# Paired retention scores, norms moved behind the gates, and the second layer's norm factor applied after its projections

## The reference, cut to what matters

```python
# block 1: retention, 8 heads, q and k 64 wide, v 128 wide, chunks of 64
y_ret = retention_chunkwise(rq, rk, rv)       # = ((q k^T) * decay) v, decay[h] over the distance
y_ret = y_ret * lax.rsqrt(jnp.mean(y_ret * y_ret, axis=-1, keepdims=True) + EPS)   # per head
y_ret = from_heads(y_ret) * ret_norm_g[layer]
y_ret = (jax.nn.silu(r_g) * y_ret) @ w_ret_out[layer]
...
# end of block 1 and start of block 2
h = h + hierarchical_moe(hn, ...)
x = rms_norm(h, norm_final_g)                 # first block's last norm
h = rmsnorm(x, norm_mix_g)                    # second block's first norm
proj = h @ w_in                               # q_nope, q_rope, c_kv, k_rope, q_idx, k_idx, w_idx, q k v of b
q_idx, k_idx, q_rope, k_rope, q_b, k_b = rope(...) of their parts
```

## Time and profile before

| | |
|---|---|
| median of 3 runs | 1814.61 us (1813.84 to 1815.03) |
| profiled execution, its own time | 1821.67 us |
| its span | 1819.9 us |
| PE busy | 1664.2 us, 91% |
| DVE, ACT, POOL busy | 898.9, 748.2, 662.7 us |
| granted clock over the span | 0.965 |
| retention on PE | 316.2 to 363.7 us of the span |
| combine, up to the first key tile | 918.7 to 981.4 us |

### The profile page before, as it was taken

The page is one execution under the profiler, slowest core; times in us unless marked ns, Lnnn a source line. Parts: engine busy times, 40 slices in busy tenths (PEclk is TensorE's granted clock), DMA queues, the critical chain, the costliest instruction groups (busy, mean ns, idle before and its releaser), DMA issues. The chain is left out here.

```text
span 1819.9 us, 21002 instructions
## 1 busy us (share of the span) xinstructions
PE 1664.2 (91%) x7928; PEld 1339.3 (74%) x7928; DVE 898.9 (49%) x1092; ACT 748.2 (41%) x886; POOL 662.7 (36%) x263
## 2 busy tenths in 40 slices
PE   4999999999999799999937989877998999999996
PEld 2888887588878788888836757644875788888885
DVE  4034211861554389989945489564333454141413
ACT  4245222343344578878823341555414322121211
POOL 2422254034444323423442625533330434444441
PEclk9999999999999899999977989988999999999998
DMA  4210152222227599999641304200130122223221
GB/s 164 96 70 24 58 162 93 67 84 92 93 97 277 220 420 392 387 393 383 266 182 60 118 25 138 96 1 1 70 139 24 70 93 93 93 96 113 92 93 46
DMA packets 46594, 249.23 MB, mean 137 GB/s; under 512 B 9440, under 2 KB 10208, under 8 KB 19904
## 3 DMA queue, kind: packets, MB, share of 16 engines
q1 hardware_dynamic: 40768, 237.85, 35.4%
q0 software_dynamic: 5184, 8.40, 1.3%
q10 hardware_dynamic: 576, 2.10, 0.3%
HBM read 238.15 MB, written 14.68 MB: 139 GB/s over the span
## 5 line engine op out<-in xcount | busy, mean ns | idle before, releaser
L148 POOL TENSOR_TENSOR w_lo<-raw,w_hi 128x2048 fp32r<-128x2048 f32 x101 | 464.8, 4603 | 745.2 <-ACT w_hi L142 745.1
L227 PE MATMUL psum<-x_hi,w_hi 128*128 128x512 f32 x872 | 346.2, 397 | 25.6 <-DVE x_lo L378 15.5
L228 PE MATMUL psum<-x_lo,w_hi 128*128 128x512 f32 x872 | 342.7, 393 | 0.0
L229 PE MATMUL psum<-x_hi,w_lo 128*128 128x512 f32 x872 | 342.4, 393 | 0.0
L142 ACT ACTIVATE w_hi<-raw 128x2048 fp32r<-128x2048 f32 x101 | 192.9, 1910 | 303.7 <-PE psum L229 303.0
L1555 DVE TENSOR_TENSOR moe_lo<-moe_w,moe_hi 128x2048 fp32r<-128x2048 f32 x99 | 225.5, 2290 | 54.5 <-ACT moe_hi L1496 53.3
L227 PEld LDWEIGHTS psum<-x_hi,w_hi 128*128 128x128 f32 x872 | 165.4, 190 | 69.2 <-DVE x_lo L378 13.3
L1496 ACT ACTIVATE moe_hi<-moe_w 128x2048 fp32r<-128x2048 f32 x99 | 189.6, 1917 | 24.0 <-PE psum L229 24.0
L229 PEld LDWEIGHTS psum<-x_hi,w_lo 128*128 128x128 f32 x872 | 165.7, 190 | 35.1
L228 PEld LDWEIGHTS psum<-x_lo,w_hi 128*128 128x128 f32 x872 | 165.9, 190 | 33.9 <-issue 0.7
L424 DVE TENSOR_TENSOR res<-res,psum 128x512 f32<-128x512 f32 x56 | 38.4, 687 | 217.6 <-PE psum L229 217.6
(11 more groups left out here) (339 smaller groups left out, 2889.4 us busy)
## 6 DMA issues: line engine op xcount, KB each, us to landing
raw<-in_w_dense SPq DMA_DIRECT2D x101, 1024.0 KB, 4.8
moe_w<-in_w_moe_ahead SPq DMA_DIRECT2D x54, 1024.0 KB, 10.6
moe_w<-in_w_moe SPq DMA_DIRECT2D x48, 1024.0 KB, 10.5
yrow<-expert_rows SPq DMA_DIRECT2D x8, 512.0 KB, 10.4
res<-in_x SPq DMA_DIRECT2D x4, 512.0 KB, 5.6
decay<-in_decay SPq DMA_DIRECT2D x8, 256.0 KB, 3.8
hn_rows<-hn_tok ACTq DMA_DIRECT2D x4, 512.0 KB, 8.5
out<-res SPq DMA_DIRECT2D x4, 512.0 KB, 2.7
```

The costliest lines, as they stand in the source:

```text
L148: pool.tensor_tensor(w_lo[c % RING][:, :], raw[c % RING][:, :], w_hi[c % RING][:, :].bitcast(F32), ALU.subtract).then_inc(lo_ready, 1)
L227: pe.matmul(out, lh, rh, start=first, stop=False)
L228: pe.matmul(out, lh, rl, start=False, stop=False)
L229: return pe.matmul(out, ll, rh, start=False, stop=last)
```

## The change

It has two parts. **Retention:** the scores of heads 2p and 2p+1 are issued together, strip by strip, one from each half of the array's rows. DVE's order becomes decayed 0 to 5, norm 0, decayed 6 and 7, norms 1 to 3; norms 4 to 7 are done after the gates of tiles 0 to 3 in `mix_vector`. `prod` gets a third buffer, every head its own root buffer; the squares take the place of cos32 and sin32, which are loaded later. The sum of squares of mem is moved behind ret_g, its matmul behind gate_ret. **Second layer:** x_hi and x_lo are made of h x g12 quarter by quarter in the combine stage, without r12. The factor r12 is multiplied in afterwards: into the rotation tables (cos_k and sin_k on DVE; cos64, sin64, cos32, sin32 on POOL), at the eviction of c_kv and of q_nope (now on DVE), and, turned to tokens on the partitions by four small matmuls, into w_eff and the eviction of v_b. The combine stage and the last stage are one block.

```diff
+    HEADS_NORMED_LATE = 4
-        def scores(h):
+        def scores(p):
-            if h >= 2:
-                pe.wait_ge(rp_done, h - 1)
+            if p >= 1:
+                pe.wait_ge(rp_done, 2 * p)
             for j in range(TB):
                 o, n = span(j)
-                mm = pe.matmul(Z[h % 2][:, o:o + n], ret_k[r:r + HD, h // 2, j * P:(j + 1) * P],
-                               ret_q[r:r + HD, h // 2, j * P:S], start=(j != 3), stop=True, skip_group_check=True)
+                for h in (2 * p, 2 * p + 1):
+                    r = HD * (h % 2)
+                    mm = pe.matmul(Z[h % 2][:, o:o + n], ret_k[r:r + HD, p, j * P:(j + 1) * P],
+                                   ret_q[r:r + HD, p, j * P:S], start=(j != 3), stop=True, skip_group_check=True)
             mm.then_inc(rs_done, 1)
...
         for h in range(HEADS):
-            if h + 1 < HEADS:
-                scores(h + 1)
+            if h % 2 == 0 and h + 2 < HEADS:
+                scores(h // 2 + 1)
             values(h)
             if h >= 1:
                 mean_square(h - 1)
...
-        for h in range(HEADS):
+        for h in range(4):
             decayed(h)
-            if h >= 2:
-                norm(h - 2)
-        norm(HEADS - 2)
-        norm(HEADS - 1)
+        decayed(4)
+        decayed(5)
+        retention_norm(dve, 0)
+        decayed(6)
+        decayed(7)
+        for h in range(1, HEADS - HEADS_NORMED_LATE):
+            retention_norm(dve, h)
...
     def mix_scalar(act):
-        norm_mem.act_sum(act, lambda e, kt: e.wait_ge(mem_landed, 16), root=False)
...
         high(KT - 1)
+        norm_mem.act_sum(act, lambda e, kt: e.wait_ge(mem_landed, 16), root=False)
...
     def mix_vector(dve):
-        dve.wait_ge(ry_done, HEADS)
-        norm_mem.vector_sum(dve, lambda e, kt: None, invert=False)
         for t in range(KT):
             dve.wait_ge(bank_free, t0 + t + 5)
+            dve.wait_ge(ry_done, t + 1)
             dve.tensor_tensor(g_tmp[t % 4][:, :], g_tmp[t % 4][:, :], ret_y[:, t, :], ALU.mult).then_inc(g_mul, 1)
             if t >= 1:
                 gated_low(t - 1)
+            if t < HEADS_NORMED_LATE:
+                retention_norm(dve, HEADS - HEADS_NORMED_LATE + t)
         gated_low(KT - 1)
+        norm_mem.vector_sum(dve, lambda e, kt: None, invert=False)
...
     def mix_tensor(pe):
         dense_pe(pe, "ret_g", x_hi, x_lo)
+        dense_pe(pe, "gate_ret", x_hi, x_lo)
         pe.wait_ge(rr_done, HEADS)
         norm_mem.pe(pe)
-        dense_pe(pe, "gate_ret", x_hi, x_lo)
...
+    def combine_vector(dve):
+        def scaled(q):
+            dve.wait_ge(yt_added, 2 * q + 2)
+            if q >= 2:
+                dve.wait_ge(xq_low, q - 1)
+            dve.tensor_tensor(hy[q % 2][:, :, :], res[:, :, q * P:(q + 1) * P], wide(g12[:, :], [P, KT, P], 2), ALU.mult)\
+               .then_inc(y_scaled, 1)
+        def low(q):
+            dve.wait_ge(y_split, q + 1)
+            dve.tensor_tensor(x_lo[:, :, q * P:(q + 1) * P], hy[q % 2][:, :, :],
+                              x_hi[:, :, q * P:(q + 1) * P].bitcast(F32), ALU.subtract).then_inc(xq_low, 1)
...
             if q >= 1:
                 add(2 * q - 2)
                 add(2 * q - 1)
+                scaled(q - 1)
+            if q >= 2:
+                low(q - 2)
         add(6)
         add(7)
+        scaled(3)
+        low(2)
+        low(3)
...
+    def combine_scalar(act):
...
+            act.wait_ge(y_scaled, q + 1)
+            act.activation(x_hi[:, :, q * P:(q + 1) * P], hy[q % 2][:, :, :], ACT.Copy).then_inc(y_split, 1)
...
     def project_sync(sp):
+        sp.wait_ge(yt_added, 2 * TB)
+        sp.wait_ge(esq_done, 2 * TB)
+        sp.wait_ge(xq_low, TB)
+        sp.dma_start(cos32[:, :], d["cos32"]).then_inc(narrow_in, 16)
+        sp.dma_start(sin32[:, :], d["sin32"]).then_inc(narrow_in, 16)
...
     def project_gpsimd(pool):
         split_lo(pool, KEYS_C + 2)
+        pool.wait_ge(r12_done, 1)
+        for table in (cos64, sin64):
+            pool.tensor_tensor(table[:, :], table[:, :], r12[:, :], ALU.mult).then_inc(tables_done, 1)
...
         dense_pool(pool, "q_nope")
+        pool.wait_ge(narrow_in, 32)
+        for table in (cos32, sin32):
+            pool.tensor_tensor(table[:, :], table[:, :], r12[:, :], ALU.mult).then_inc(tables_done, 1)
...
     def project_scalar(act):
-        norm3.act_split(act)
-        act.wait_ge(tile_done, KEYS_T + 1)
-        act.activation(c_kv[:, :], psum[:, KEYS_T % 4, :], ACT.Copy)
-        act.activation(kv_sq[:, :], psum[:, KEYS_T % 4, :], ACT.Square).then_inc(bank_free, 1)
+        act.wait_ge(bank_free, KEYS_T + 5)
+        act.activation(kv_sq[:, :], c_kv[:, :], ACT.Square).then_inc(kv_squared, 1)
...
-        dense_act(act, "q_nope", q_nope)
+        dense_act(act, "q_nope")
...
     def project_vector(dve):
-        norm3.vector_split(dve, ready=lambda: None)
         dve.wait_ge(proj_in, 80)
+        dve.wait_ge(r12_done, 1)
+        for table in (cos_k, sin_k):
+            ins = dve.tensor_tensor(table[:, :], table[:, :], r12[:, :], ALU.mult)
+        link(dve, ins)
+        dve.wait_ge(bank_free, KEYS_T + 4)
+        dve.wait_ge(tile_done, KEYS_T + 1)
+        dve.tensor_tensor(c_kv[:, :], psum[:, KEYS_T % 4, :], r12[:, :], ALU.mult).then_inc(bank_free, 1)
...
+        for j in range(4):
+            t = FIRST_TILE["q_nope"] + j
+            dve.wait_ge(tile_done, t + 1)
+            dve.tensor_tensor(q_a[0:HD, 2 * j, :], psum[0:HD, t % 4, :], r12[0:HD, :], ALU.mult)
+            dve.tensor_tensor(q_a[HD:P, 2 * j + 1, :], psum[HD:P, t % 4, :], r12[HD:P, :], ALU.mult).then_inc(bank_free, 1)
...
     def project_tensor(pe):
-        norm3.wait_split(pe, 1)
+        pe.wait_ge(xq_low, TB)
...
         dense_pe(pe, "q_idx", x_hi, x_lo)
+        pe.wait_ge(kv_squared, 1)
         pe.matmul(psum[:, 4, :], ones[:, :], kv_sq[:, :], start=True, stop=True).then_inc(kv_steps, 1)
...
+        for q in range(TB):
+            mm = pe.matmul(psum[:, 5, 64 + q:65 + q], r12[:, q * P:(q + 1) * P], ident[:, 0:1], start=True, stop=True,
+                           skip_group_check=True)
```

More of the change, by code:

```diff
@@ L455, in build @@
     norm1 = Norm("norm1", res, "mix", 170, hi=x_hi, lo=x_lo)
-    CONSTS = [("ident", ident), ("neg_tri", neg_tri), ("before", before), ("cos64", cos64), ("sin64", sin64),
-              ("cos32", cos32), ("sin32", sin32)]
+    CONSTS = [("ident", ident), ("neg_tri", neg_tri), ("before", before), ("cos64", cos64), ("sin64", sin64)]
     cols_landed = sem("cols_landed")
@@ new lines, in combine_vector, with add @@
+    def combine_vector(dve):
+        def add(n):
+            q, half = n // 2, n % 2
+            dve.wait_ge(yt_done, n + 1)
+            r4 = res[:, 4 * half:4 * half + 4, q * P:(q + 1) * P]
+            dve.tensor_tensor(r4, r4, psum[:, 1 + n % 4, :].rearrange("p (k n) -> p k n", n=P), ALU.add)\
+               .then_inc(yt_added, 1)
+        def scaled(q):
[8 more added lines that the diff above has]
+                              x_hi[:, :, q * P:(q + 1) * P].bitcast(F32), ALU.subtract).then_inc(xq_low, 1)
+        g1, g2 = (cols[:, COLS[n]:COLS[n] + KT] for n in ("end1", "mix2"))
+        link(dve, dve.tensor_tensor(g12[:, :], g1, g2, ALU.mult))
+        for q in range(TB):
+            dve.wait_ge(yrows_landed[q], 32)
+            dve.tensor_scalar(ysum[:, q, :], yrow[0][q][:, :], gates2[:, 0, q:q + 1], None, ALU.mult).then_inc(ys1, 1)
+            dve.wait_ge(ys1, q + 1)
+            dve.scalar_tensor_tensor(out=ysum[:, q, :], in0=yrow[1][q][:, :], scalar=gates2[:, 1, q:q + 1],
+                                     in1=ysum[:, q, :], op0=ALU.mult, op1=ALU.add).then_inc(ys2, 1)
+            if q >= 1:
+                add(2 * q - 2)
+                add(2 * q - 1)
+                scaled(q - 1)
+            if q >= 2:
+                low(q - 2)
+        add(6)
+        add(7)
+        scaled(3)
+        low(2)
+        low(3)
+        dve.wait_ge(esum_sq, 2 * TB)
+        link(dve, dve.tensor_scalar(esum[:, :], psum[:, 5, :], EPS / D, EPS * EPS, ALU.mult, ALU.add))
+        dve.scalar_tensor_tensor(out=esum[:, :], in0=psum[:, 6, :], scalar=1.0 / D, in1=esum[:, :],
+                                 op0=ALU.mult, op1=ALU.add).then_inc(esum_done, 1)
+        dve.wait_ge(eroot, 1)
+        dve.reciprocal(r12[:, :], r12_inv[:, :]).then_inc(r12_done, 1)
@@ new lines, in combine_tensor, with sums @@
+    def combine_tensor(pe):
+        def sums(q):
+            for m in range(2):
+                pe.wait_ge(esq_done, 2 * q + m + 1)
+                for kt in range(KT):
+                    mm = pe.matmul(psum[:, 5 + m, q * P:(q + 1) * P], ones[:, :], esq[m][:, kt, :],
+                                   start=(kt == 0 and q == 0), stop=(kt == KT - 1), skip_group_check=True)
+                mm.then_inc(esum_sq, 1)
+        for n in range(2 * TB):
+            q, half = n // 2, n % 2
+            pe.wait_ge(ys2, q + 1)
+            if n >= 4:
```

(21 more changed lines are left out.)

193 lines of the change are left out of this document (74 added, 119 removed).

## The result

The changed kernel takes 1806.3 us, the median of 12 runs (1801.59 to 1810.24). The kernel before, in 12 runs of its own, takes 1819.36 (1813.8 to 1822.9). The ratio is 0.9929, 95% interval [0.9915, 0.9944]: 0.71% or 13 us faster, between 10 and 15.5. Forecast were 1805.8 us and 8.85 us of gain. The time was met to 0.5 us, the gain was not: the three runs of before that the forecast started from lay 4.7 us under the median of the twelve, and the change gave 4 us more than the sum.

The account below looks back on a forecast made before the run. TensorE, busy 91% of the span, was taken as the bound; other work counts only where it waits for it or works on it. 3.4 + 0.6 - 1.4 - 1.7 + 9.3 - 1.35 = 8.85 us gained: 1805.8, range 1800.5 to 1811.5.

Parts of the forecast that it names:

- Retention, 3.4: Retention: paired scores at 2.42 us a pair, less new idle places on PE, end it 3.4 us earlier.
- ret_g, 0.6: ret_g: ACT no longer starts it behind the squares of mem, so PE's 0.6 us wait goes.
- gate_ret, -1.4: Start of gate_ret: squares of mem delay ACT's evictions and weight split, so PE waits; 1.4 us lost.
- The dip, -1.7 of 0 to 3.4: Retention: PE's clock falls after the new 3.4 us gap; 1.7 us lost, bounds 0 and 3.4.
- the gap before the third pair: Retention: PE idles 0.85 us before scores(2), as the decay tables of heads 2 and 3 load late.
- Combine, 9.3: Combine and keys: x no longer waits for the norm factor, so q_idx starts 9.3 us earlier.
- Index stage, -1.35: Index stage: earlier weight split gains 1.15 us, POOL's cos32 and sin32 products lose 2.5; net 1.35 lost.
- POOL's first copy: Combine, a rival: POOL's hg(0) wins the port against DVE's scale(0); 1.8 us later, 1807.6 us; chance 0.15.
- The factor: Keys, a rival: norm factor r12 still binds through ACT's queue; at 3.5 us late, 1807.7 us; chance 0.1.
- Rival 3: Retention: paired scores run one after the other; 1814.6 us, no change; chance 0.05.
- rival 4: Retention: seven gaps hold PE at 1.2 GHz, so the kernel is slower, up to 1839.5 us; chance 0.03.
- rival 5: No dip in retention, or cos32 products fall into pauses: 1804.1 or 1803.3 us, both 1801.6; chance 0.12.

Follow-up runs that it names:

- unpaired: The changed kernel with the two heads' scores of a pair issued one head after the other; 1816.05 us, ratio 0.9983 to the kernel before.
- mem_between: The changed kernel with the memory's squares and adds put two to a tile into ret_g's loop; 1806.81 us, ratio 0.9929 to the kernel before.
- ret_only: The kernel before with only the new retention and ret_g, layer two as before; 1815.23 us, ratio 0.9985 to the kernel before.
- factor_late: The changed kernel with the norm factor's reciprocal done twice in a row; 1808.61 us, ratio 0.9943 to the kernel before.
- tables_late: The changed kernel with POOL's two narrow table products moved behind its index masks; 1805.56 us, ratio 0.9926 to the kernel before.

## Why the prediction was right, and where its sizes were off

The gain came by the steps laid out, and their sum was 4.2 us too small. That the time was met to 0.5 us is luck: the median of three runs under it was 4.7 us too low.

**Retention, 3.4:** measured 3.37 in the profile without a dip. Pairs at one half's price, gaps of 3.37, 0.98 and four times 0.98 at the places named, DVE's norms no limit: all as laid out. unpaired confirms that a pair costs 2.43 us only by its order; single file costs 4.00, not the 4.84 taken as the other bound.

**ret_g, 0.6, and gate_ret, -1.4:** measured 0.65 and 1.38; mem_between takes the latter away and so shows its cause.

**The dip, -1.7 of 0 to 3.4:** the mechanism is right and the step mis-sized. 0 in two profiles of eleven, 0.7 in six, 1.7 to 2.0 in three, 0.9 on average. I added it to the gap before the third pair; in truth the dip fills that gap.

**Combine, 9.3:** 10.6 against the profile of before, 7.6 against ret_only's. Counted from the first yrow load, the last sum came 46.5 us later where I had 47.5 to 48.3; the order at the port was the one laid out by hand, within 0.6 us up to the end of the second weight split and 1.35 us early at the last x_lo. So the layout was mis-sized by about 1.3. But the base is less certain than that: the same stretch of the old code took 45.1 us in before and 42.0 in ret_only, and I had taken before's clock loss of 2.8 us in the last sums as part of the stage. From the last sum on every distance was met. To wi it is 23.0 us in both profiles of the old code and 10.9 in all eleven of the new one whose factor is not delayed, and wi to q_idx is 7.24. Those 12.1 us are the mechanism; what the longer combine stage takes back is 1.5 us against before and 4.5 against ret_only.

**Behind q_idx, nothing in the sum:** 1.6 us gained, the step that was missing. The same wait of 1.83 us stands before q_idx in both kernels. In before it was followed by 0.87, in the changed kernel by 1.00. ret_only, with layer two as before, has the fall as well (20.15 us from wi to the first rotated tile). Of the other profiles with the new layer two, unpaired (20.20) and factor_late (19.86) have it, and the other nine do not (18.5 to 18.7). In the changed kernel PE was busy for 12.00 of 12 us at 1.00 in the key tiles (the window above), where before had 8.64 at 0.61; that this is the reason was not tested, and unpaired, with the same code there, speaks against it as the whole of it. It stays open.

**Index stage, -1.35:** -1.29 (0.49 gained, 1.78 lost; I had 1.15 and 2.5). tables_late gives back 1.67, so the products' place is the cause.

**Rivals.** POOL's first copy did not win the port: both started within 0.06 us of each other and DVE's took 1.23. The factor did not bind, and factor_late shows how near it is: 2.15 us. Rival 3 is out by unpaired, rival 4 by the eleven retentions, none over 45.1 us. Of rival 5, the dip was absent in two of eleven.

In sum, by the profiles: 2.5 (retention with its average dip) - 0.7 + 10.6 + 1.6 - 1.3 = 12.7, against 8.85 forecast and 13.1 between the medians. With ret_only's combine stage as the base it is 9.7. The runs allow 10 to 15.5. Of what the forecast lacked, 1.6 behind q_idx and 0.8 of the dip show in both readings; the 1.3 of the combine stage hang on the one profile of before.

## What to carry to other kernels

When two engines share a port, write their order down instruction by instruction: the record's length then tells who waited. Here the layout came out 1.35 us long in 45. Before such a difference is explained, look at how much the same code varies: this stage differed by 3 us between two profiles of the old code and by 2.5 among ten of the new. When work is moved off the path, give its cover a number and try it by making the work longer by a known amount; what is left of that amount tells the cover. And a stall that follows a clock dip can be free, as the 0.98 us before the third pair were, so don't add both.

A change of 3 us can't be read from six runs of this kernel, whose runs spread over 4 to 12 us while their code stays the same, in part by the clock of stages that no edit touched. Read by stage, two edits of 1.6 us each were plain in one profile.

## What the runs showed of the hardware

Matmuls of 64 rows in alternate halves of the array, in FP32: 16 in 2.43 us, against 4.00 to 4.03 one half after the other. A single head's eight took 2.42 before the next kind of matmul started, so two heads in single file are cheaper than twice that.

Between DVE and POOL the port changed hands at each instruction: DVE, blocked by POOL's split, got it before POOL's next instruction (5.47 us for a copy of 1.23), and then POOL before DVE's next (2.88 us, of which 1.75 came after DVE's end). The Trainium skill, SBUF — State Buffer, Who interferes with whom, says of DVE's two-port modes that whoever issues first gets the pair for the whole instruction and the other fully blocks. The rows show the same for DVE instructions with two SBUF inputs, and add that a waiting engine comes before the next instruction of the one that held it.

In or just behind one wait of 3.37 us the clock fell to its low level in nine profiles of eleven with the same instructions around it, for 3.4 us in six and 6.8 us in three, and stayed at 1.00 in two. In unpaired it fell for 10.2 us.
